# An encoder layer with 32 experts: six of twelve residual tiles stay on chip, and the ring of expert weights has eight places in place of ten

## Chip, cores, metric

The kernel runs on one NeuronCore of a Trainium2 chip. The metric is device time in microseconds (us) of one execution. All matrix work is in float32; where the code says "split", a float32 matrix is taken apart into a rounded part (hi, type fp32r) and the rest (lo), and three products of such parts stand for the one product.

## The reference, cut down

One layer of an encoder is applied to two sequences of 512 and 1024 tokens with 1024 features (1536 tokens, twelve tiles of 128). It is a mixer, a cross-attention to a memory, and a mixture of experts, each added to a residual h:

```python
h = x
h = h + parallel_mixer(rmsnorm(h, g_mix), ...)
h = h + memory_cross_attention(rmsnorm(h, g_xattn), ...)
h = h + hierarchical_moe(rmsnorm(h, g_moe), ...)
return rmsnorm(h, g_final)

def hierarchical_moe(hn, w_rg, w_re, w_gate, w_up, w_down):
    # top-1 of 4 groups, then top-2 of its 8 experts, 32 experts in all
    hg = jnp.einsum('nd,edf->nef', xf, w_gate)     # each expert 1024 x 128
    hu = jnp.einsum('nd,edf->nef', xf, w_up)       # 1024 x 128
    act = jax.nn.silu(hg) * hu * gates[..., None]
    out = jnp.einsum('nef,efd->nd', act, w_down)   # 128 x 1024
```

## The kernel before

All stages up to the experts leave the residual in one SBUF buffer, `H = at(0, NT, D)`: twelve tiles of 4 KB in each partition, at 0 to 48 KB, tile t at 4t KB. After the cross-attention's output is added to tile t, that tile is normalised (`norms` of kind "moe"), stored as rows to DRAM (`xn_moe`), turned and put through the router. When all twelve are through, a table of rows is made, and the experts begin.

**Expert blocks.** Each of the 32 experts first gets one block of up to 128 rows. Rows that did not fit go to overflow blocks afterwards; this input needs seven of them. POOL gathers the rows of block b from `xn_moe` into a ring of `RING = 6` places and scatters the result of block b to `y_tok` in DRAM. In each of the first 32 blocks TensorE runs, in this order, the turning of the next block's rows (L2280), 24 matmuls for gate and up (L571 to L573), `down(b - 1)` (L2314), and the turning of the activation (L2307). ScalarE, in block e - 1, makes the hi part of expert e's gate and up weights (`split_expert`, two instructions of L561), and only behind that comes `silu(e - 1)` (L1323). VectorE makes the lo part of the first half, waits for the silu, multiplies (L1867), and makes the lo part of the second half (L566). `gate_up(e)` on TensorE waits for that last lo part.

**The ring of weights.** Expert e uses place e % `W_RING`. A place holds 12 KB in each partition: gate and up, 8 KB, and down, 4 KB. Three DMAs of 512 KB fill it, all from SyncE's queue (SP), all counted on one semaphore of the place, and `split_expert` waits for all three:

```python
act.wait_ge(w_e_here[e % W_RING], 48 * (e // W_RING + 1))
```

Where the places lie overlaps with other buffers: of the ten, those at 0, 12, 24 and 36 KB lie on H (three tiles each). Experts 0 to 9 are loaded ahead of the expert stage, each as soon as what its place overlaps is done with. From then on the loop in the SP program reloads a place when its reader is done: gate and up when `gate_up` of the place's former expert has ended (`gu_done`), down when its `down` has (`y_done`). SP works strictly in its program's order. Every overflow block loads the weights of its expert again, into the place that `OVER_SLOTS` names, once `down` of the block six before it is done.

**Kept rows.** Since weights overwrite H, SP first copies each tile of H to DRAM (`keep_rows`, L793, `h_kept`), and reads all twelve back after the overflow loads (L850), for the final stage, which adds the experts' rows (`y_tok`, two per token, with their gates) to H and does the last RMSNorm, some tiles on VectorE and some on TensorE.

Of the kernel before, what the change touches and what calls it, by code (L numbers as in the profile page):

```python
# [11 lines left out]
P = 128  # L12
D = 1024
KT = D // P
SEQ_P, SEQ_S = 512, 1024
T = SEQ_P + SEQ_S
NT = T // P
# [28 lines left out]
NBLK = NE + NOVER  # L46
TG = 4
RING = 6
W_RING = 10
OVER_SLOTS = (2, 6, 8, 9, 0, 1)  # L50
AHEAD = 6
EARLY = 4
N_EARLY = 2 * EARLY * P
# [6 lines left out]
def hymba_encoder(nc, a, y_prompt, y_sample):  # L60
    ctx = ExitStack()
    with ctx:
        def sem(name):
            return ctx.enter_context(nc.semaphore(name))
# [6 lines left out]
        def at(kb, *shape, dt=F32):  # L71

            used[0] += 1
            base = nc.sbuf_base + (-nc.sbuf_base) % 32
            return nc.alloc_sbuf_tensor_at(f"at_{kb}_{used[0]}".replace(".", "_"), [P, *shape], dt, offset=base + int(kb * 1024))[:]
# [3 lines left out]
        def dram(name, shape, dt=F32):  # L79
            return nc.dram_tensor(name, shape, dt, kind="Internal").ap()  # L80
# [4 lines left out]
        rpb_pad = dram("rpb_pad", [NH * 15, 96])  # L85
        xn_moe = dram("xn_moe", [T, D])
        y_tok = dram("y_tok", [N_EARLY + 2 * T, D])
        h_kept = dram("h_kept", [T, D])
        xT_hi_all, xT_lo_all = dram("xT_hi_all", [P, KT, T]), dram("xT_lo_all", [P, KT, T])


# [47 lines left out]
        H = at(0, NT, D)  # L139
# [74 lines left out]
        iota_p = at(187, P)  # L214
        iota_blk = at(187.5, NBLK)

        slots_kb = [48, 60, 108, 0, 12, 24, 84, 36, 72, 96]
        w_gu = [at(kb, 2, KT, FE) for kb in slots_kb]
        w_gu_lo = [at(kb, 2, KT, FE, dt=F32R) for kb in slots_kb]
        w_dn = [at(kb + 8, D) for kb in slots_kb]  # L220
# [60 lines left out]
        n_sq, n_eps, n_rs, n_ready, nt_done, nt_evac = (sem(n) for n in ("n_sq", "n_eps", "n_rs", "n_ready", "nt_done", "nt_evac"))  # L281
        xn_stored = [sem(f"xn_stored_{n}") for n in range(4)]
        h_moved = sem("h_moved")
# [8 lines left out]

        w_e_here = [sem(f"w_e_here_{n}") for n in range(W_RING)]
        xg_here = [sem(f"xg_here_{n}") for n in range(RING)]
        xgt_done, xg_hi, xg_lo, gu_done, e_silu, e_act, act_turned, act_evac, y_done, y_evac_s, y_evac_v = (
            sem(n) for n in ("xgt_done", "xg_hi", "xg_lo", "gu_done", "e_silu", "e_act", "act_turned", "act_evac",
                             "y_done", "y_evac_s", "y_evac_v"))
# [30 lines left out]
        TPC = CH // P  # L328
# [103 lines left out]
        for k, st in enumerate(stages):  # L432
            ready = [("pre", n) for n in range(4, len(norms)) if pre_at[n] == k]
            order += [("sq", n) for n in range(4, len(norms)) if sq_at[n] == k]
            if st[0] == "T" and norms[st[1]][0] == "h":
                t = norms[st[1]][1]
# [22 lines left out]
        n_norms = {g: n for n, g in enumerate(norms)}  # L459
# [18 lines left out]
        def overflow_blocks(eng, body):  # L478

            used = eng.value_load(over_n[0:1, 0:1], min_val=0, max_val=NOVER)  # L480
            with eng.Fori(0, NOVER // RING) as i:
                with ExitStack() as nested:
                    for n in range(RING):
                        nested.enter_context(eng.If(used > RING * i + n))
                        body(NE + RING * i + n, n % 2, n, i, NE // 2 + RING // 2 * i + n // 2)

        def over_weights(n, i):

            slot = OVER_SLOTS[n]
            return slot, len(range(slot, NE, W_RING)) + i  # L490

# [115 lines left out]
        def _(sp):  # L607
# [165 lines left out]
            def load_gate_up(e, n):  # L773
                one = slice(e, e + 1) if isinstance(e, int) else bass.ds(e, 1)
                sp.dma_start(w_gu[n][:, 0], a["w_exp_gate"][0, one].rearrange("e (p k) f -> p (e k) f", p=P)).then_inc(w_e_here[n], 16)
                sp.dma_start(w_gu[n][:, 1], a["w_exp_up"][0, one].rearrange("e (p k) f -> p (e k) f", p=P)).then_inc(w_e_here[n], 16)

            def load_down(e, n):
                one = slice(e, e + 1) if isinstance(e, int) else bass.ds(e, 1)
                sp.dma_start(w_dn[n], a["w_exp_down"][0, one].rearrange("e p d -> (e p) d")).then_inc(w_e_here[n], 16)  # L780
# [9 lines left out]

            def keep_rows(t):
                sp.wait_ge(mm_evac, n_groups["xo", t, 1] + 1)
                sp.dma_start(h_kept[t * P:(t + 1) * P], H[:, t]).then_inc(h_moved, 16)  # L793

            def load_expert(e):
                load_gate_up(e, e % W_RING)
                load_down(e, e % W_RING)

# [1 line left out]
                for row in (N_EARLY + k * T, k * EARLY * P):  # L800
                    sp.dma_start(y_tok[row:row + EARLY * P], a["x_prompt"][0][0:EARLY * P]).then_inc(y_filled, 16)

            for t in range(2 * TPC):
                keep_rows(t)
            sp.wait_ge(mm_done, n_groups["o", NCH - 1, XH - 1] + 1)
            for e in range(3):
                load_expert(e)
            sp.wait_ge(h_moved, 16 * 2 * TPC)
            sp.wait_ge(n_ready, n_norms["moe", 2] + 1)
            load_expert(3)  # L810
            sp.wait_ge(n_ready, n_norms["moe", 5] + 1)
            load_expert(4)
            keep_rows(8)
            sp.wait_ge(h_moved, 16 * 9)
            sp.wait_ge(n_ready, n_norms["moe", 8] + 1)
            load_expert(5)
            for t in (9, 10, 11):
                keep_rows(t)
            sp.wait_ge(mm_done, n_groups["xo", NT - 1, 1] + 1)
            load_expert(6)  # L820
            sp.wait_ge(h_moved, 16 * NT)
            sp.wait_ge(n_ready, n_norms["moe", 11] + 1)
            load_expert(7)
            sp.wait_ge(mm_done, len(groups))
            for j in range(4):
                sp.wait_ge(xn_stored[j], 16 * NT // 4)
            load_expert(8)
            load_expert(9)


            for e in range(W_RING, NE):
                sp.wait_ge(gu_done, e - W_RING + 1)
                load_gate_up(e, e % W_RING)
# [11 lines left out]
                load_down(e, slot)  # L845

            overflow_blocks(sp, load_overflow)
            sp.wait_ge(y_done, 28)
            for t in range(NT):
                sp.dma_start(H[:, t], h_kept[t * P:(t + 1) * P]).then_inc(h_moved, 16)  # L850
            sp.dma_start(gf_row, a["g_final"].partition_broadcast(P)).then_inc(consts_here, 16)

            def load_y(t):
# [518 lines left out]
        def _(dve):  # L1372
# [301 lines left out]
            for what, n in order:  # L1674
# [10 lines left out]
                elif what == "pre":  # L1685
                    dve.wait_ge(n_rs, n + 1)
                    kind, t = norms[n]
# [6 lines left out]
                elif what == "T":  # L1694
                    kind, t = norms[n]
# [10 lines left out]
                elif what == "mm":  # L1706
# [3 lines left out]
                    if kind == "xo":  # L1710
                        t, half = which
# [189 lines left out]


            dve.wait_ge(consts_here, 16 * 7)
            dve.wait_ge(h_moved, 16 * 2 * NT)

            def add_experts(t):
                y_landed(dve, t)
# [31 lines left out]
        def _(pe):  # L1939
# [226 lines left out]
            for what, n in stages:  # L2166
# [28 lines left out]
                elif what == "mm":  # L2195
# [31 lines left out]
                    elif kind == "xo":  # L2227
                        t, half = which
# [6 lines left out]
                    else:  # L2235
                        t = which[0]
# [7 lines left out]
                elif what == "S":  # L2244
                    c, t, hp = n // 8, (n % 8) // 2, n % 2
# [89 lines left out]
            pe.wait_ge(table_ready, 4)  # L2335
            overflow_blocks(pe, overflow)

            pe.wait_ge(h_moved, 16 * 2 * NT)
            for m, t in enumerate(BY_PE):
                if m >= 3:  # L2340
                    pe.wait_ge(f_out, with_halves(BY_PE[m - 3]))
# [38 lines left out]
```

## Time and profile before

| what | value |
|---|---|
| median of 3 runs | 1213.64 us (1212.94 to 1214.68) |
| the profiled execution's own time | 1212.87 us |
| its span, first to last instruction | 1211.2 us |
| mean granted TensorE clock | 0.981 of full speed |
| TensorE matmuls busy | 1139.3 us, 94% of the span |
| VectorE, ScalarE, GpSimd busy | 642.2, 470.1, 234.6 us |
| moved by DMA | 226.59 MB |

The span is the profiled execution's instructions from first to last; 1.7 us of its time lie outside. Times of events in the text below are counted from the start of the span. The stretches that matter here are: cross-attention and routing up to about 914, expert blocks 0 to 31 from 915 to 1108, seven overflow blocks to 1159, the final stage to 1211. Busy shares average over stages with different limits; which wait ends last has to be read from each stage.

### The profile page before, as it was taken

The numbers are of one execution on the slowest core, as the hardware profiler recorded it, in microseconds if no ns is written. First come the engines' busy times: TensorE is split into PE (matmuls) and PEld (weight loads), VectorE is DVE, ScalarE is ACT, GpSimd is POOL, SyncE is SP. The second block draws the span as 40 slices with busy tenths as digits, with TensorE's granted clock in tenths as the row PEclk, the third lists the DMA queues.
The fourth block names the chain that finished last, engine by engine and source line by source line (L and its number), as shares of the span: only waits on it lengthen the run. The fifth ranks groups of instructions, "written<-read, shape, count | busy, mean of one in ns | idle before, by whom it ended". The sixth has DMA issues, their size and how long they took to land.

```text
span 1211.2 us, 18987 instructions
## 1 busy us (share of the span) xinstructions
PE 1139.3 (94%) x6854; PEld 912.2 (75%) x6854; DVE 642.2 (53%) x1244; ACT 470.1 (39%) x982; POOL 234.6 (19%) x337
## 2 busy tenths in 40 slices
PE   6999999999998999999999999999986999999956
PEld 5888888878885666888898787778775788887732
DVE  6333333212116896323565663754577998885256
ACT  6233333211015785111332433544224666774223
POOL 3322322200000001000100100100022334454344
PEclk9999999999999999999999999999996999999979
DMA  9573553833158425523222001912796999989967
GB/s 318 133 256 114 145 166 96 296 93 95 46 113 218 110 53 180 174 73 94 62 75 70 1 11 73 317 70 92 307 343 246 373 369 354 357 299 355 406 257 272
DMA packets 108428, 226.59 MB, mean 187 GB/s; under 512 B 28854, under 2 KB 48318, under 8 KB 108222
## 3 DMA queue, kind: packets, MB, share of 16 engines
q1 hardware_dynamic: 83822, 167.86, 40.9%
q0 software_dynamic: 17856, 43.02, 10.8%
q10 hardware_dynamic: 6672, 14.69, 3.8%
q8 instruction: 47, 0.77, 0.3%
q14 instruction: 31, 0.25, 0.1%
HBM read 180.89 MB, written 69.78 MB: 207 GB/s over the span
## 4 chain that ended last, share of the span: by engine, by line
PE 85%; DMA 3%; DVE 3%; ACT 2%; issue 2%; SPq 2%; POOL 1%; DVEq 0%; POOLq 0%; ACTq 0%
PE bank L571 18%; PE bank L573 18%; PE bank L572 18%; PE bank L2314 6%; PE bank L2242 3%; PE bank L2280 3%; PE bank L2111 3%; PE bank L2097 2%; PE bank L2084 2%; PE bank L2300 2%; PE bank L2251 2%; PE bank L2176 1%; DMA at<-v_att 1%; PE bank L1946 1%; PE bank L2022 1%
## 5 line engine op out<-in xcount | busy, mean ns | idle before, releaser
L571 PE MATMUL bank<-at,at 128*128 128x512 f32 (+1 forms) x1192 | 441.1, 370 | 5.3 <-DVE at L566 2.8
L573 PE MATMUL bank<-at,at 128*128 128x512 f32 (+1 forms) x1192 | 431.0, 362 | 0.0
L572 PE MATMUL bank<-at,at 128*128 128x512 f32 (+1 forms) x1192 | 430.5, 361 | 0.0
L571 PEld LDWEIGHTS bank<-at,at 128*128 128x128 f32 x1192 | 225.6, 189 | 40.8 <-DVE at L566 3.6
L573 PEld LDWEIGHTS bank<-at,at 128*128 128x128 f32 x1192 | 225.4, 189 | 34.6
L572 PEld LDWEIGHTS bank<-at,at 128*128 128x128 f32 x1192 | 225.8, 189 | 32.2
L566 DVE TENSOR_TENSOR at<-at,at 128x1024 fp32r<-128x1024 f32 (+2 forms) x162 | 180.7, 1129 | 104.3 <-ACT at L561 101.6
L561 ACT ACTIVATE at<-at 128x1024 fp32r<-128x1024 f32 (+2 forms) x162 | 154.4, 988 | 167.9 <-DVE at L1522 49.0
L894 POOL TENSOR_TENSOR at<-at 128x1 f32<-128x1 f32 x88 | 24.2, 275 | 557.9 <-ACT at L1253 282.3
L2314 PE MATMUL bank<-at,at 128*128 128x512 f32 x156 | 74.2, 597 | 3.3 <-ACT at L1327 3.3
L990 POOL DMA_INDIRECT y_tok<-at,at x39 | 39.5, 1013 | 133.0 <-DVE at L1872 99.0
L983 POOL DMA_INDIRECT at<-xn_moe,at x45 | 59.6, 1324 | 21.5 <-issue 20.8
L1166 ACT ACTIVATE at<-at,at 128x256 f32<-128x256 f32 (+1 forms) x96 | 51.4, 537 | 29.3 <-DVE at L1490 29.1
L896 POOL TENSOR_TENSOR at<-at 128x1 f32<-128x1 f32 x88 | 55.0, 625 | 6.9
L2280 PEld LDWEIGHTS bank<-at,at 128*128 128x128 f32 x320 | 40.5, 193 | 14.0 <-issue 8.0
L1490 DVE CUSTOM_DVE_ANT_0 at<-bank,at 128x256 f32<-128x256 f32 (+1 forms) x96 | 41.1, 466 | 18.0 <-PE bank L2084 17.4
L2280 PE MATMUL bank<-at,at 128*128 128x128 f32 x320 | 44.0, 282 | 7.1 <-DMA at<-xn_moe,at 5.6
L1856 DVE TENSOR_TENSOR at<-bank,at 128x512 fp32r<-128x512 f32 x64 | 41.3, 685 | 12.8 <-ACT at L1314 12.7
L1332 ACT ACTIVATE at<-bank 128x512 f32<-128x512 f32 x39 | 23.3, 598 | 62.9 <-PE bank L2314 56.0
L2097 PEld LDWEIGHTS bank<-at,at 128*128 128x128 f32 x224 | 24.0, 142 | 28.0 <-ACT at L1166 25.1
L2314 PEld LDWEIGHTS bank<-at,at 128*128 128x128 f32 x156 | 26.7, 190 | 24.0 <-issue 18.8
L2242 PE MATMUL bank<-at,at 128*128 128x36 f32 (+1 forms) x240 | 43.8, 339 | 0.0
(215 smaller groups left out, 1316.2 us busy)
## 6 DMA issues: line engine op xcount, KB each, us to landing
at<-in_w_exp_gate SPq DMA_DIRECT2D x39, 512.0 KB, 7.3
at<-in_w_exp_up SPq DMA_DIRECT2D x39, 512.0 KB, 10.3
at<-in_w_exp_down SPq DMA_DIRECT2D x39, 512.0 KB, 12.7
at<-y_tok SPq DMA_DIRECT2D x24, 512.0 KB, 10.4
at<-in_w_in SPq DMA_DIRECT2D x6, 1024.0 KB, 11.5
xT_hi_all<-at POOLq DMA_DIRECT2D x12, 512.0 KB, 3.9
xT_lo_all<-at POOLq DMA_DIRECT2D x12, 512.0 KB, 5.7
at<-xT_hi_all SPq DMA_DIRECT2D x3, 2048.0 KB, 10.1
```

The lines of the kernel that those rows point to most:

```text
L561: nc.scalar.activation(hi, x, ACT.Copy).then_inc(hi_made, 1)
L566: nc.vector.tensor_tensor(lo, x, hi.bitcast(F32), ALU.subtract).then_inc(lo_made, 1)
L571: nc.tensor.matmul(out, w_hi, x_hi, start=(k == 0), stop=False)
L572: nc.tensor.matmul(out, w_lo, x_hi, start=False, stop=False)
L573: last = nc.tensor.matmul(out, w_hi, x_lo, start=False, stop=(k == len(terms) - 1))
L896: pool.tensor_tensor(rs[:, col:col + 1], ms_eps[:, col:col + 1], neg_half, ALU.pow).then_inc(out_sem, 1)
L983: pool.indirect_dma_start(out=x_g[b % RING], out_offset=None, in_=xn_moe, in_offset=bass.IndirectOffsetOnAxis(ap=slot_src[:, b:b + 1], axi ...
L1166: nc.scalar.activation(p, p, ACT.Exp, bias=na_st[:, 2 * (s % 2) + n:2 * (s % 2) + n + 1], scale=-1.0, accum_out=na_st[:, 4 + 2 * (s % 2) + ...
L2097: last = nc.tensor.transpose(bank[4 + n][:, k * P:(k + 1) * P], na_p[s % 2][:, n, k * P:(k + 1) * P], ident)
L2242: mm = nc.tensor.matmul(b if kind == "route" else b[:], w, x, start=(k == 0), stop=(k == len(steps) - 1))
L2280: mm = nc.tensor.transpose(bank[k // 4][:, (k % 4) * P:(k % 4 + 1) * P], x_g[n].rearrange("p (q k) -> p k q", k=KT)[:, k], ident)
L2314: mm = nc.tensor.matmul(bank[5 + k][:], act_T[j], w_dn[slot][:, k * HALF:(k + 1) * HALF], start=True, stop=True)
```

## The change

H stays where it is. Its tiles 0 to 5 (0 to 24 KB) are no longer overlapped by weights: the places at 0 and 12 KB are gone, and eight are left. The copies of tiles 0 to 5 to DRAM and back go with them. Ahead of the expert stage eight experts are loaded instead of ten. The copy of tile 8, of which SP waited behind five loads, now stands behind three.

```diff
-W_RING = 10
-OVER_SLOTS = (2, 6, 8, 9, 0, 1)
+W_RING = 8
+OVER_SLOTS = (0, 1, 2, 4, 6, 7)
+KEPT = 6
...
-        h_kept = dram("h_kept", [T, D])
+        h_kept = dram("h_kept", [T - KEPT * P, D])
...
-        slots_kb = [48, 60, 108, 0, 12, 24, 84, 36, 72, 96]
+        slots_kb = [48, 60, 108, 24, 84, 36, 72, 96]
...
-            for t in range(2 * TPC):
+            for t in range(KEPT, 2 * TPC):
                 keep_rows(t)
             sp.wait_ge(mm_done, n_groups["o", NCH - 1, XH - 1] + 1)
             for e in range(3):
                 load_expert(e)
-            sp.wait_ge(h_moved, 16 * 2 * TPC)
-            sp.wait_ge(n_ready, n_norms["moe", 2] + 1)
+            keep_rows(8)
+            sp.wait_ge(h_moved, 16 * (9 - KEPT))
+            sp.wait_ge(n_ready, n_norms["moe", 8] + 1)
             load_expert(3)
-            sp.wait_ge(n_ready, n_norms["moe", 5] + 1)
-            load_expert(4)
-            keep_rows(8)
-            sp.wait_ge(h_moved, 16 * 9)
-            sp.wait_ge(n_ready, n_norms["moe", 8] + 1)
-            load_expert(5)
             for t in (9, 10, 11):
                 keep_rows(t)
             sp.wait_ge(mm_done, n_groups["xo", NT - 1, 1] + 1)
-            load_expert(6)
-            sp.wait_ge(h_moved, 16 * NT)
+            load_expert(4)
+            sp.wait_ge(h_moved, 16 * (NT - KEPT))
             sp.wait_ge(n_ready, n_norms["moe", 11] + 1)
-            load_expert(7)
+            load_expert(5)
             sp.wait_ge(mm_done, len(groups))
             for j in range(4):
                 sp.wait_ge(xn_stored[j], 16 * NT // 4)
-            load_expert(8)
-            load_expert(9)
+            load_expert(6)
+            load_expert(7)
...
-            sp.wait_ge(y_done, 28)
-            for t in range(NT):
-                sp.dma_start(H[:, t], h_kept[t * P:(t + 1) * P]).then_inc(h_moved, 16)
+            sp.wait_ge(y_done, 30)
+            for t in range(KEPT, NT):
+                sp.dma_start(H[:, t], h_kept[(t - KEPT) * P:(t - KEPT + 1) * P]).then_inc(h_moved, 16)
...
-            dve.wait_ge(h_moved, 16 * 2 * NT)
+            dve.wait_ge(h_moved, 16 * 2 * (NT - KEPT))
...
-            pe.wait_ge(h_moved, 16 * 2 * NT)
+            pe.wait_ge(h_moved, 16 * 2 * (NT - KEPT))
```

## Rows read from the trace of the kernel before

**Rows 1.** The page: each engine's busy us, its share of the span, instructions.
```profile
PE 1139.3 (94%) x6854; PEld 912.2 (75%) x6854; DVE 642.2 (53%) x1244; ACT 470.1 (39%) x982; POOL 234.6 (19%) x337
```

**Rows 2.** Windows: engines' busy us, then granted clock, DMA share, GB/s.
```profile
855.00:884.00 29.00, 27.06 (x169) 23.93 (x170) 17.95 (x53) 6.68 (x13) 1.49 (x4) 1.00 0.93 362
...
930.00:960.00 30.00, 29.24 (x189) 23.10 (x188) 27.99 (x46) 19.76 (x36) 7.74 (x8) 1.00 0.81 300
960.00:990.00 30.00, 30.00 (x204) 25.00 (x204) 28.09 (x48) 20.59 (x37) 10.70 (x11) 1.00 1.02 387
...
1020.00:1050.00 30.00, 30.00 (x205) 24.94 (x203) 25.63 (x37) 21.62 (x38) 15.38 (x12) 1.00 0.95 365
...
1066.00:1080.00 14.00, 14.00 (x89) 10.97 (x88) 11.78 (x15) 9.07 (x17) 7.83 (x6) 1.00 0.84 316
1080.00:1090.00 10.00, 10.00 (x73) 8.72 (x72) 8.06 (x12) 7.83 (x14) 5.44 (x4) 1.00 0.68 247
1090.00:1106.00 16.00, 16.00 (x110) 13.24 (x109) 11.88 (x16) 9.08 (x17) 8.18 (x7) 1.00 0.98 348
```

**Rows 3.** Timeline of SP's queue: start us, us of issuing, line, transfer.
```profile
930.15 0.33 SPq L775 DMA_DIRECT2D at<-in_w_exp_gate  x1
...
1035.39 4.81 SPq L780 DMA_DIRECT2D at<-in_w_exp_down  x1
...
1058.79 2.10 SPq L780 DMA_DIRECT2D at<-in_w_exp_down  x1
1060.93 2.30 SPq L775 DMA_DIRECT2D at<-in_w_exp_gate  x1
...
1065.45 1.21 SPq L780 DMA_DIRECT2D at<-in_w_exp_down  x1
1085.81 0.35 SPq L775 DMA_DIRECT2D at<-in_w_exp_gate  x1
```

**Rows 4.** DMA issues, landing us last: down 1035.39; down 1058.79 and 1065.45; gate 1060.93.
```profile
at<-in_w_exp_down SPq DMA_DIRECT2D x1, 512.0 KB, 26.9
...
at<-in_w_exp_down SPq DMA_DIRECT2D x1, 512.0 KB, 24.5
...
at<-in_w_exp_gate SPq DMA_DIRECT2D x1, 512.0 KB, 9.4
```

**Rows 5.** Timeline of ACT, DVE and PE around the weights of experts 24 and 31.
```profile
1059.35 2.03 ACT L561 ACTIVATE at<-at 128x1024 fp32r<-128x1024 f32 x2
...
1098.46 2.03 ACT L561 ACTIVATE at<-at 128x1024 fp32r<-128x1024 f32 x2
1100.72 0.28 ACT L1323 ACTIVATE at<-bank 128x128 f32<-128x128 f32 x1 [0.23 <-PE bank L573]
...
1101.23 1.22 DVE L566 TENSOR_TENSOR at<-at,at 128x1024 fp32r<-128x1024 f32 x1
...
1103.16 0.36 PE L571 MATMUL bank<-at,at 128*128 128x256 f32 x1
```

**Rows 6.** SP around the copy of tile 8: its timeline row, and SP's waits.
```profile
863.56 1.77 SPq L793 DMA_DIRECT2D h_kept<-at  x1
...
SPq L775 <- DMA h_kept<-at: 18.4, 2, 16.9
```

**Rows 7.** Overflow: down loads issued about 1086.73 and 1103.48, landing; chain's first overflow matmuls.
```profile
at<-in_w_exp_down SPq DMA_DIRECT2D x1, 512.0 KB, 10.0
...
at<-in_w_exp_down SPq DMA_DIRECT2D x1, 512.0 KB, 12.7
...
1110.83 3.45 PE bank L2300 x16
...
1117.81 3.45 PE bank L2300 x16
```

**Rows 8.** Reading H back: timeline of SP's queue, and the window of 1150 to 1155.
```profile
1120.79 11.84 SPq L850 DMA_DIRECT2D at<-h_kept  x12
...
1150.00:1155.00 5.00, 5.00 (x19) 3.66 (x20) 0.91 (x2) 0.60 (x1) 1.18 (x2) 1.00 0.62 237
```

More of the change, by code:

```diff
@@ L792, in keep_rows @@
                 sp.wait_ge(mm_evac, n_groups["xo", t, 1] + 1)
-                sp.dma_start(h_kept[t * P:(t + 1) * P], H[:, t]).then_inc(h_moved, 16)
+                sp.dma_start(h_kept[(t - KEPT) * P:(t - KEPT + 1) * P], H[:, t]).then_inc(h_moved, 16)
             def load_expert(e):
```

## The prediction

> **What bounds the kernel now.** I read the page first: TensorE is busy for 94% of the span [rows 1]. Then the windows. From 960 to 1106 TensorE has no idle time at all, so an expert block costs what its matmuls cost: the weights of experts 24 and 31 are split at 1059.35 and 1098.46, seven blocks apart, 5.59 us each [rows 5]. The same windows show the second thing to see: DMA is at a share of 0.95 to 1.02 and 365 to 387 GB/s for most of that time [rows 2]. So the expert stage is bound by TensorE with DMA just below it, and what keeps DMA hidden is the lead of the weight loads. I looked at that lead in the timeline of SP's queue and in the landing times [rows 3, 4].
>
> Expert 27's down load is issued at 1035.39 and lands 26.9 us later, at 1062.3. Those of 30 and 31 are issued at 1058.79 and 1065.45 and land 24.5 us later, at 1083.3 and 1090.0. That is (1090.0 - 1062.3) / 4 = 6.9 us for an expert's weights, and 6.7 for the last one, against 5.59 us for a block of TensorE. The stream of weights is slower than its reader, and the kernel lives on the lead that ten places give.
>
> The deadline of the last expert is worked out backwards from the timeline [rows 5]. `gate_up(31)` starts at 1103.16. VectorE's last lo part for it ends at 1101.23 + 1.22 = 1102.45, 0.7 us sooner. ScalarE's split of expert 31 starts at 1098.46 and ends at 1100.49, and the silu behind it starts 0.23 us later only because TensorE is not done. So the weights may land 0.7 + 0.2 = 0.9 us after 1098.46, at 1099.4, before anything moves. They land at 1090.0: the lead is 9.4 us, less than two blocks. Experts 28, 29, 30 have deadlines 5.59 us apart: 1082.6, 1088.2, 1093.8.
>
> **The change part by part.**
>
> *Six writes and six reads of H go.* Each is 0.524 MB, 3.15 MB each way. The writes were issued during cross-attention, where nothing of TensorE's chain waits for them. The twelve reads are issued from 1120.79 on, under overflow blocks that TensorE fills, and DMA already falls to a share of 0.62 at 1150 to 1155, before the final stage [rows 8]. What is taken away was hidden at both ends: 0 us. If that cover were gone, 3.15 MB at 365 GB/s would be 8.6 us each way.
>
> *Two loads fewer ahead of the experts.* The old loads of experts 3 and 4 vanish from the stretch of 855 to 884 [rows 2]. The copy of tile 8 was issued at 863.56, and SP waited up to 16.9 us for it [rows 6]. It is now behind three loads instead of five, and lands up to 3.15 MB / 362 GB/s = 8.7 us sooner. Behind that wait stand the load of expert 3 and the copies of tiles 9 to 11. They may start sooner, but expert 3 isn't split until four blocks in, so the gain is nothing. All that follows (experts 4 to 7 in place of 6 to 9) keeps the same waits on TensorE and VectorE, so the first gather meets the same queue: 0 us.
>
> *The moved stream.* In the loop the load of e waits for expert e - 8 instead of e - 10. The first is issued by the same event as before, the end of `gate_up(0)` at 930.15 [rows 3]; it was expert 10 and is now expert 8. From there on the SP program issues the same bytes on the same events, with the numbers moved by two, and gathers and scatters beside them are unchanged. So I take the landing times of before and give them to experts two lower: 28 lands when 30 did, 29 when 31 did. The last two, 30 and 31, have no forerunner. They follow without a pause, since DMA was left idle only after this point (share 0.84 and then 0.68 [rows 2], with SP issuing nothing from 1065.45 to 1085.81 [rows 3]). At 6.7 us each they land at 1096.7 and 1103.4, at 6.9 at 1096.9 and 1103.8.
>
> Against the deadlines: expert 28 at 1083.3 - 1082.6 = 0.7 us late, 29 at 1090.0 - 1088.2 = 1.8, 30 at 2.9 to 3.1, 31 at 4.0 to 4.4. Lateness does not add up, since one late block moves all later deadlines; the last one is the stall, 4.2 us in all, in four pieces of about 1 us. When TensorE waits, its gathers and scatters wait too. They are what is left of the 365 GB/s after 1.57 MB in 6.9 us, 228 GB/s: 137 GB/s, or 0.4 us of DMA given back for each us of stall. With about 2 us stalled ahead of the last landing that is 0.7 us. Sum: 4.2 - 0.7 = +3.5 us. Bounds: below, 0, if the last two loads fit wholly in the idle share; above, 4.4 without relief and up to about 6 if the pace is 7.6 us for the last two.
>
> At the same load, gate lands 9.4 us after its issue and down 24.5 [rows 4], although gate of expert 31 is issued after down of expert 30: landing is not in order of issue. The Trainium skill ("DMA: Bandwidth & Descriptors", "Why a DMA increments its semaphore by 16 and not by 1") says that a DMA runs on up to 16 engines that finish independently, and that only the full count means all has landed. By the 9.4 us, expert 31 would be there long before 1099.4 and the sum would be 0; by the last of the three, which is what `split_expert` waits for, it is +3.5. The rows of the down loads decide, and I take the second.
>
> *Overflow.* `OVER_SLOTS` names other places, but each load waits for the same `y_done` as before. The first overflow load, at 1085.81, landed by about 1096.7, and its matmuls started at 1110.83 [rows 3, 7]. Now it queues behind expert 31: 1103.5 + 6.7 = 1110.2, against 1110.8 + 3.5 = 1114.3. The margin shrinks from 14 us to 4 us, but TensorE takes 7.0 us for such a block (1110.83 to 1117.81 [rows 7]), as long as a load needs, so it isn't used up. 0 us. The wait `y_done` 30 in place of 28 stands behind the last overflow load, which needed 33 already.
>
> *Final stage.* Its bytes before the end: two experts (3.15 MB) later, six reads (3.15 MB) fewer. Even: 0 us.
>
> The profiled execution would go from 1212.87 to 1216.4. The median lies 0.8 us above it, so 1213.64 + 3.5 = 1217.1 us.
>
> **The rivals.** What measurement can tell from no change is 0.2%, 2.4 us.
>
> *The two loads fit in the gap: no change.* From 1066 to 1090 DMA has idle share of 0.16 x 14 + 0.32 x 10 = 5.4 us [rows 2], and by bytes at the 387 GB/s of 960 to 990 two experts need 8.1 us: 1090.0 + 8.1 = 1098.1, in time for 1099.4. With up to 1 us of stall at 28 and 29 it stays at 1213.6 to 1215. Against it: the pace of 6.7 to 6.9 us at full share is that of the same bytes with gathers beside them. The Trainium skill (same page, "Bandwidth") measured 425 GB/s for a core that streams alone; by it two experts would take 7.4 us and be in time too. No window of the expert loop shows it; the most there is 387.
>
> *More than the last four: the overflow loads come late as well.* Their margin is 4 us. If landings spread by 2 us more for each of the last two experts, both the stall and the overflow blocks take it: 3.5 + 4 = about 1221. For it: landing grew from 10.0 to 12.7 us even behind an idle queue [rows 7]. Against it: gathers end as overflow begins.
>
> *Faster.* Ahead of the experts DMA runs at 0.93 from 855 to 884 [rows 2], with stores of `xn_moe` in the same engines, and TensorE is idle for 1.9 us there. If those idle times hang on late stores and loads, taking 3.15 MB out gives up to 1.9 us: 1211.7. It decides only if the last experts land in time too. Nothing in that stretch is shown waiting for DMA except SP itself.
>
> **How the numbers follow.** Forecast 0.61, at 1217.1, own range 1215.2 to 1219. No change 0.24. Overflow late too 0.09. Faster 0.06. The forecast's lower edge falls within 0.2% about one time in twenty. So slower 0.67, same 0.26, faster 0.07. The range of 8 in 10 reaches down into "no change" and up towards the third case: 1213.3 to 1220.3.
>
> **What would show it.** In the changed kernel: DMA share near 1 from 1066 to 1090; ScalarE's L561 waiting for `at<-in_w_exp_down` in the blocks of experts 28 to 31, PE idle for 3 to 4 us in about 1080 to 1110, none before; the loads of 30 and 31 landing near 1097 and 1103; the first overflow matmul near 1114; the stretch before 930 unchanged. Wrong would be: no idle PE in the loop; idle PE in earlier blocks, which would mean that the stream isn't the old one moved by two; or a changed stretch before 930.

## The result and the profile after

| what | before | changed |
|---|---|---|
| median of 22 runs each | 1213.62 us (1211.96 to 1217.95) | 1216.17 us (1212.41 to 1220.13) |
| ratio of the two | | 1.002, interval 1.0012 to 1.0027 |
| the profiled execution | 1212.87 us, span 1211.2 | 1215.17 us, span 1213.3 |
| moved by DMA | 226.59 MB | 220.30 MB |

The changed kernel is slower by 2.5 us, 0.2%, where the prediction had 3.5 us; its median lies in the forecast's own range (1215.2 to 1219). It moves 6.29 MB less and is still slower. The page of the changed kernel, its span, busy times and bytes, against [rows 1]:

```profile
span 1213.3 us, 18973 instructions
...
PE 1140.6 (94%) x6854; PEld 913.1 (75%) x6854; DVE 643.9 (53%) x1244; ACT 470.5 (39%) x982; POOL 228.1 (19%) x337
...
DMA packets 106701, 220.30 MB, mean 182 GB/s; under 512 B 28663, under 2 KB 48127, under 8 KB 106495
```

TensorE does the same work in a span that is 2.1 us longer. The windows say where DMA is used otherwise, with the columns of [rows 2]:

```profile
855.00:884.00 29.00, 26.85 (x168) 23.76 (x169) 17.93 (x53) 6.87 (x13) 1.48 (x4) 1.00 0.88 326
930.00:960.00 30.00, 29.24 (x189) 23.03 (x187) 27.86 (x46) 19.70 (x37) 7.59 (x8) 1.00 0.84 301
...
1066.00:1080.00 14.00, 14.00 (x89) 11.01 (x89) 11.68 (x16) 9.21 (x17) 7.96 (x6) 1.00 1.00 361
1080.00:1090.00 10.00, 10.00 (x73) 8.71 (x72) 6.82 (x10) 6.67 (x12) 4.05 (x4) 1.00 0.92 354
1090.00:1106.00 16.00, 15.34 (x97) 11.76 (x96) 12.46 (x17) 10.78 (x20) 4.05 (x4) 1.00 0.95 335
```

From 1066 to 1090, DMA's share was 0.84 and 0.68; it is 1.00 and 0.92. The idle room is filled, and TensorE has idle time behind it, 16 - 15.34 = 0.66 us from 1090 to 1106. Since the ends of matmuls are modelled, short idle times can be missing there; ScalarE's timeline shows the stall more sharply. These are the splits of experts 28 to 31, one row each:

```profile
1082.11 2.01 ACT L562 ACTIVATE at<-at 128x1024 fp32r<-128x1024 f32 x2
...
1089.10 2.00 ACT L562 ACTIVATE at<-at 128x1024 fp32r<-128x1024 f32 x2 [1.52 <-DMA at<-in_w_exp_down]
...
1095.46 2.00 ACT L562 ACTIVATE at<-at 128x1024 fp32r<-128x1024 f32 x2 [1.89 <-DMA at<-in_w_exp_down]
...
1101.12 2.01 ACT L562 ACTIVATE at<-at 128x1024 fp32r<-128x1024 f32 x2 [1.18 <-DMA at<-in_w_exp_down]
```

Undisturbed they would stand 5.59 us apart, at 1087.4, 1093.0 and 1098.6 for the last three. The waits of 925 to 1115 that end on a weight load or on the split behind it (us in total, number, longest):

```profile
DVE at L567 <- ACT at L562: 5.7, 5, 2.0
ACT at L562 <- DMA at<-in_w_exp_down: 4.6, 3, 1.9
```

The kernel before has no wait of ScalarE for `in_w_exp_down` there. A word on that name: the three loads of a place count on one semaphore, 16 counts each, and the profile gives the first 16 counts to gate, the next to up and the last to down, in the order of issue. So the landing that it prints for a down load is the moment of the 48th count, when all three are there, and that is what the split waits for. The landing printed for gate is only the 16th of the 48 counts, whichever loads they came from.

SP's queue shows the loads moved (against [rows 3]), and the landings behind three of its rows are 27.1 us for the down load of expert 29, 24.4 for expert 30 and 23.9 for expert 31:

```profile
930.29 0.33 SPq L776 DMA_DIRECT2D at<-in_w_exp_gate  x1
...
1061.94 4.73 SPq L781 DMA_DIRECT2D at<-in_w_exp_down  x1
...
1071.08 1.84 SPq L781 DMA_DIRECT2D at<-in_w_exp_down  x1
...
1077.17 1.87 SPq L781 DMA_DIRECT2D at<-in_w_exp_down  x1
1085.95 0.35 SPq L776 DMA_DIRECT2D at<-in_w_exp_gate  x1
```

So 29 lands at 1061.94 + 27.1 = 1089.0, 30 at 1095.5, 31 at 1101.1, each at the start of its split. Last, the chain: the first overflow matmuls and the last ones of the final stage, against [rows 7]:

```profile
1112.51 3.45 PE bank L2296 x16
...
1199.11 3.45 PE bank L2348 x8
```

The first was at 1110.83: +1.68. The last was at 1196.89: +2.2 (2.1 in the span). These 2.2 us are: 0.15 us that the expert stage begins later, 1.5 us of stall at experts 29 to 31, 0.1 in the overflow blocks, 0.45 in the final stage.

**How profiles are compared below.** The stretch ahead of the experts varies from one execution to the next: the loop's first load is issued between 929.2 and 932.1 in the twelve profiles, against 930.15 in that of the kernel before. So each profile is given its shift: the start of the split of expert 12 (990.97 in the kernel before, 991.12 in the changed one, shift +0.15). The stall in the loop is the first overflow matmul minus 1110.83 minus the shift. The ratios take in all runs of both kernels and are not the quotient of the two medians.

### The profile page after: what moved, and what is told of

Same layout as the page of the kernel before. It is cut to its first block, busy times and chain, and to the rows that moved or that the text cites. A ratio compares the mean times of both kernels' runs of the same rounds, so it can differ in the third digit from the quotient of the medians.

```text
span 1213.3 us, 18973 instructions
## 1 busy us (share of the span) xinstructions
PE 1140.6 (94%) x6854; PEld 913.1 (75%) x6854; DVE 643.9 (53%) x1244; ACT 470.5 (39%) x982; POOL 228.1 (19%) x337
## 2 busy tenths in 40 slices
DMA packets 106701, 220.30 MB, mean 182 GB/s; under 512 B 28663, under 2 KB 48127, under 8 KB 106495
## 4 chain that ended last, share of the span: by engine, by line
PE 84%; DMA 4%; issue 3%; ACT 2%; DVE 2%; SPq 2%; POOL 1%; DVEq 0%; POOLq 0%; ACTq 0%
PE bank L572 18%; PE bank L574 17%; PE bank L573 17%; PE bank L2310 5%; PE bank L2238 3%; PE bank L2107 3%; PE bank L2276 2%; PE bank L2093 2%; PE bank L2080 2%; DMA at<-in_w_exp_down 2%; PE bank L2296 2%; PE bank L2247 2%; PE bank L2348 2%; PE bank L2172 2%; DMA at<-y_mix 1%
## 5 line engine op out<-in xcount | busy, mean ns | idle before, releaser
L979 POOL DMA_INDIRECT at<-xn_moe,at x45 | 55.6, 1236 | 21.5 <-issue 21.2
```

Of the source, the lines that this page charges most:

```text
L979: pool.indirect_dma_start(out=x_g[b % RING], out_offset=None, in_=xn_moe, in_offset=bass.IndirectOffsetOnAxis(ap=slot_src[:, b:b + 1], axi ...
```

## The experiments

The theory (A, where the expectations use letters): the lead of the weight loads is what eight places take away. The stall comes where the last landing of an expert's three loads passes the deadline of its split. The copies of H are worth nothing to either end. Against it stand: the copies count (ahead of the experts or in the final stage), or it is not the lead but the load of DMA in the loop.

**The number of places.** Nine places, three tiles kept (the loads ahead of the experts follow suit):

```diff
-W_RING = 8
-OVER_SLOTS = (0, 1, 2, 4, 6, 7)
-KEPT = 6
+W_RING = 9
+OVER_SLOTS = (5, 7, 8, 0, 1, 2)
+KEPT = 3
...
-        slots_kb = [48, 60, 108, 24, 84, 36, 72, 96]
+        slots_kb = [48, 60, 108, 12, 24, 84, 36, 72, 96]
```

> Nine places for expert weights, tiles 0 to 2 stay in SBUF, tiles 3 to 11 are copied out and read back. Theory A (the cost is the lead of the weight stream): the last expert lands one item of the stream later than with ten places, near 1095.5 in place of 1090.0, and the deadline of its split is 1099.4. So there is no stall: no idle TensorE in blocks 25 to 31, the first overflow matmul at 1111, and a time within 0.5 us of the kernel before. Theory B (the cost comes with the number of places or copies changed, by other placement or other traffic): half the change gives half the cost, +1.3 us.

Measured: 1213.24 us against 1212.77 of the kernel before on the same chip, ratio 1.0006 (0.9996 to 1.0015). ScalarE does not wait for weights, and the first overflow matmul is at 1110.36 with shift -0.47: stall 0. One place fewer is covered by the lead.

Seven places, with only tiles 6 to 8 copied:

```diff
-W_RING = 8
-OVER_SLOTS = (0, 1, 2, 4, 6, 7)
+W_RING = 7
+OVER_SLOTS = (4, 5, 6, 0, 1, 2)
...
-        slots_kb = [48, 60, 108, 24, 84, 36, 72, 96]
+        slots_kb = [48, 60, 108, 24, 84, 72, 96]
...
-            for t in range(KEPT, NT):
+            for t in range(KEPT, KEPT + 3):
```

> Seven places, tiles 0 to 5 and 9 to 11 stay in SBUF, only 6 to 8 are copied out and read back. Theory A: the stream goes on for one more item of about 5.6 to 6.4 us behind the landing at 1101.1, so expert 31 lands near 1107, and TensorE stalls about 5 us more than with eight places, in the blocks from about expert 27 on, less the relief from gathers and scatters that wait too: +6 to +8 us against the kernel before. Theory B, in proportion to the places: 3/2 of 2.5 us, +3.8 us; if fewer copies gave something back, less.

Measured: 1218.61 us, ratio 1.0044 (1.0028 to 1.0059). Its wait for weights in the same stretch, and three of the rows of ScalarE's timeline:

```profile
ACT at L562 <- DMA at<-in_w_exp_down: 10.3, 6, 3.0
```

```profile
1064.28 2.00 ACT L562 ACTIVATE at<-at 128x1024 fp32r<-128x1024 f32 x2 [2.87 <-DMA at<-in_w_exp_down]
...
1089.63 2.00 ACT L562 ACTIVATE at<-at 128x1024 fp32r<-128x1024 f32 x2 [3.02 <-DMA at<-in_w_exp_down]
...
1105.68 2.01 ACT L562 ACTIVATE at<-at 128x1024 fp32r<-128x1024 f32 x2
```

The stall begins at expert 23 (its split at 1056.93) instead of 29, and the last two splits are in time again. First overflow matmul at 1117.83, shift +1.8: 5.2 us in the loop. From ten to seven places the medians are 0, +0.5 (not told from nothing), +2.5 and +5.8 us. That the cost starts only at the eighth is what a lead with a threshold gives, and not what a cost per byte gives.

**Is it the wait for the down load?** Eight places, but down is counted on semaphores of its own, `split_expert` waits for gate and up alone, and `down` waits for its own load:

```diff
...
-                act.wait_ge(w_e_here[e % W_RING], 48 * (e // W_RING + 1))
+                act.wait_ge(w_e_here[e % W_RING], 32 * (e // W_RING + 1))
...
-            def down(b, j, slot):
+            def down(b, j, slot, n_loads):
+                pe.wait_ge(w_d_here[slot], w_d_base[slot] + 16 * (n_loads + 1))
```

> Eight places as in the changed kernel, but the down weights are counted on semaphores of their own, and the split of gate and up waits for those two alone; the matmul for down waits for its own. Theory A: gate and up of expert 31 are issued some 2 to 5 us ahead of down and land 2 to 4 us ahead of it, so the splits of experts 29 to 31 start on time; down itself is needed 8 us later than the split. ScalarE no longer waits for a weight load, TensorE is idle 0 to 0.5 us in the loop, and the time is that of the kernel before, within 0.8 us. Theory B (traffic or placement): no difference from the changed kernel, +2.5 us. If the landing is spread so much between DMA engines that gate and up come as late as down, A gives +2 us as well, and the profile shows ScalarE still waiting.

Measured: 1214.19 us, ratio 1.0015 (1.0003 to 1.0028), where the changed kernel stands at 1.002 (1.0012 to 1.0027). The intervals overlap, so the times alone do not tell the two kernels apart; the profile does. It has the span (1211.2) and the first overflow matmul (1110.83) of the kernel before, shift 0: no stall. What is left of the wait:

```profile
ACT at L564 <- DMA at<-in_w_exp_up: 0.9, 2, 0.6
```

Gate and up still keep the splits of experts 29 and 30 waiting, 0.2 and 0.6 us, which the 0.9 us of slack take up. The split of expert 31 begins at 1099.23 instead of 1098.46, after a wait that the profile gives to no load: 0.1 us more would have been a stall. Gate and up of expert 30 are there at 1093.61, where all three loads were at 1095.46 in the changed kernel. What was gained by not waiting for down is 1.3 and 1.7 us at experts 29 and 30, less the shifts, just enough here.

The same with SP's order by need, gate and up of e + 1 ahead of down of e:

```diff
...
-            for e in range(W_RING, NE):
-                sp.wait_ge(gu_done, e - W_RING + 1)
-                load_gate_up(e, e % W_RING)
-                sp.wait_ge(y_done, e - W_RING + 1)
-                load_down(e, e % W_RING)
+            for e in range(W_RING, NE + 1):
+                if e < NE:
+                    sp.wait_ge(gu_done, e - W_RING + 1)
+                    load_gate_up(e, e % W_RING)
+                if e > W_RING:
+                    sp.wait_ge(y_done, e - W_RING)
+                    load_down(e - 1, (e - 1) % W_RING)
```

> Eight places, down counted apart, and SyncE issues gate and up of expert e + 1 ahead of down of expert e, so that gate and up stand 0.5 MB further ahead in the stream, 2 us at its pace. Theory A (the cost is the lead of what the split waits for): ScalarE waits 0 to 0.3 us for weights, the first overflow matmul at 1110.8, and the median within 0.8 us of the kernel before, at or below the one with down merely apart, whose ScalarE still waited 0.9 us for up and whose median was 1.4 us above before. Down of expert 31 now lands last, near 1101, and is needed near 1106, so it adds nothing. Theory B, that what remained in that run was something else than waits for weights: again +1.4 us.

Measured: 1213.65 us against 1213.10, ratio 0.9999 (0.999 to 1.0008). No wait of ScalarE for weights at all; first overflow matmul at 1109.88, shift -0.97: stall 0. With the same eight places and the same bytes, the cost is gone. So the cause is the lead, the time between the landing that the split waits for and the split's deadline, and not the number of places in itself. How much of it is the count and how much the order is not shown: the new order also lets SP finish issuing sooner, its last load of the loop at 1071.68 instead of 1080.08 with down merely apart, and the order alone was not tried.

**The changed kernel once more**, beside the last one on the same chip:

> The changed kernel itself once more, on the same chip as the next three, so that small differences to them are not differences of chips. Both theories: +2 to +3 us against the kernel before; in the profile ScalarE waits for at<-in_w_exp_down at the splits of experts 29 to 31, 4 to 5 us in all, and the first overflow matmul starts 1.5 to 2 us later than at 1110.8.

Measured: 1215.54 us, ratio 1.0017 (1.0008 to 1.0025). Its final stage is as long as that of the kernel before. Its stall is smaller, 1112.62 - 1110.83 - 0.97 = 0.8 us, and so are its waits:

```profile
ACT at L562 <- DMA at<-in_w_exp_down: 3.5, 3, 1.6
```

**The copies.** Eight places with all twelve tiles copied and read back (`KEPT = 0`, nothing else differs from the changed kernel):

> Eight places as in the changed kernel, but all twelve tiles are copied out and read back as before. Theory A (copies hidden at both ends): the same as the changed kernel, +2.5 us. In the changed kernel the overflow weights land up to 8 us later than before (1139 in place of 1131), so the six more reads, 3.15 MB or 8 us, may reach into the start of the final stage: then up to +5 us. Theory B in the form that the copies of tiles 0 to 5 cost time in the kernel before, hidden in the balance: clearly over +2.5 us, with the loss in the stretch before 930.

Measured: 1219.23 us, ratio 1.0058 (1.0044 to 1.0072), +6.5 us where the changed kernel had +2.5. The loop is that of the changed kernel (first overflow matmul 1112.40, shift -0.36: stall 1.9 us). What differs is the end. SP's queue, VectorE's first row of the final stage, and windows of 1150 to 1160:

```profile
1124.67 14.54 SPq L846 DMA_DIRECT2D at<-h_kept  x12
...
1140.41 11.27 SPq L854 DMA_DIRECT2D at<-y_tok  x8
```

```profile
1167.55 0.87 DVE L1825 TENSOR_SCALAR at<-at,at 128x128 f32<-128x128 f32 x4 [6.23 <-DMA y_tok<-at,at]
```

```profile
1150.00:1155.00 5.00, 4.63 (x22) 3.31 (x21) 1.67 (x3) 1.68 (x4) 0.69 (x1) 1.00 1.01 390
1155.00:1160.00 5.00, 4.63 (x23) 3.22 (x21) 0.98 (x2) 1.15 (x3) 2.03 (x2) 1.00 0.49 189
```

The same rows of the changed kernel:

```profile
1125.71 7.03 SPq L846 DMA_DIRECT2D at<-h_kept  x6
...
1133.96 11.41 SPq L854 DMA_DIRECT2D at<-y_tok  x8
```

```profile
1165.16 0.87 DVE L1825 TENSOR_SCALAR at<-at,at 128x128 f32<-128x128 f32 x4 [3.73 <-DMA y_tok<-at,at]
```

```profile
1150.00:1155.00 5.00, 4.63 (x23) 3.27 (x22) 1.67 (x3) 1.68 (x4) 0.80 (x1) 1.00 0.33 123
1155.00:1160.00 5.00, 4.63 (x23) 3.33 (x21) 0.98 (x2) 1.15 (x3) 2.02 (x2) 1.00 0.12 40
```

And that of the kernel before:

```profile
1163.39 0.87 DVE L1829 TENSOR_SCALAR at<-at,at 128x128 f32<-128x128 f32 x4 [3.63 <-DMA y_tok<-at,at]
```

In the kernel with all copies and the changed one, the last scatter is issued at nearly the same time (1162.17 and 1162.29). With twelve reads the `y_tok` loads start 6.45 us later and DMA is still full at 1155; VectorE starts the final stage 2.4 us later after a wait that is 2.5 us longer, and the last matmuls are at 1202.20 instead of 1199.11: 3.1 us. So with eight places, in which the overflow weights land late, the six reads are worth about 3 us.

Is that so without the stall too? The ordered kernel with `KEPT = 0`:

> Eight places with down apart and the order changed (no stall in the loop), but all twelve tiles copied out and read back. It separates the two costs of the run with eight places and all copies, +6.5 us. If the six more reads push the final stage, as its profile suggests (VectorE's first instruction of that stage 2.4 us later, and 0.7 us more up to the end), this run has no stall in the loop and +2.5 to +4 us in all. If that run's extra cost hung on the stall, this one gives the time of the kernel before.

Measured: 1215.88 us against 1212.52, ratio 1.0025 (1.0016 to 1.0034), against 0.9999 with six reads. No wait of ScalarE for weights; first overflow matmul at 1112.37, shift +1.53: stall 0. The final stage begins late again:

```profile
1166.79 0.87 DVE L1829 TENSOR_SCALAR at<-at,at 128x128 f32<-128x128 f32 x4 [5.38 <-DMA y_tok<-at,at]
```

Less the shift that is 1165.26, 1.9 us later than in the kernel before, and the last matmuls, at 1201.14, are 2.7 us later less the shift. The price of the reads needs no stall, only the stream moved by two.

Now the writes alone. Ten places; the copies of tiles 0 to 5 aren't written, and the rows of tiles 6 to 11 are read back in their place, so the residual of six tiles is left out of the result. SP's waits on `h_moved` follow suit:

```diff
...
-            for t in range(2 * TPC):
+            for t in range(6, 2 * TPC):
                 keep_rows(t)
...
-                sp.dma_start(H[:, t], h_kept[t * P:(t + 1) * P]).then_inc(h_moved, 16)
+                sp.dma_start(H[:, t], h_kept[(t % 6 + 6) * P:(t % 6 + 7) * P]).then_inc(h_moved, 16)
```

> The kernel before without the copies of tiles 0 to 5 to DRAM; all twelve are still read back, for tiles 0 to 5 the rows of tiles 6 to 11 are read, so the residual of tiles 0 to 5 is wrong in the result. It shows what six writes cost ahead of the experts. My theory: nothing, 0.0 us, within what can be told (0.2%), since no wait of TensorE's chain ends with them. The other: up to 1.9 us faster, the idle time of TensorE from 855 to 884, if late stores cause it.

Measured: 1213.45 us against 1213.10, ratio 1.0001 (0.9991 to 1.0011). The writes cost nothing ahead of the experts, to within 1.3 us. With that falls the rival that taking them out makes the kernel faster.

**Ten places and more bytes.** If all that counts is when weights land, ten places must stall too, once the stream is late by as much. Six DMAs of 512 KB, from one place in DRAM to another, behind the down loads of experts 25 to 30:

```diff
...
+                if 25 <= e < 31:
+                    n = e - 25
+                    sp.dma_start(spare[n * P:(n + 1) * P], a["x_sample"][0][n * P:(n + 1) * P]).then_inc(y_filled, 16)
```

> The kernel before, with ten places and all its copies, and six more transfers of 512 KB (DRAM to DRAM, a part of x to a spare tensor) from SyncE's queue, one behind each down load of experts 25 to 30: the 3.15 MB that the change moves into the loop, without the shorter lead. Expert 31 then lands near 1098 in place of 1090, against a deadline of 1099.4. Theory A: in the loop 0 to 0.5 us. The same bytes also push the overflow weights and the reading back of H later, as in the run with all copies, so the final stage may start 0 to 3 us late: +0 to +3 us in all, with none of it before 1110. Theory C (bytes in the loop cost by themselves, whatever the lead): a stall in the loop of 1.5 us or more before the first overflow matmul, as in the changed kernel. A copy within DRAM may hold the DMA engines longer than a load; then the last weights come after 1099.4 and some stall shows for A too.

Measured: 1219.56 us against 1213.10, ratio 1.0037 (1.0022 to 1.0051); four of its six runs are near 1219.6 and two near 1216, so its median says little. It stalled more than was meant, for expert 31 landed 6 us later than the 1098 that was expected:

```profile
1095.64 2.00 ACT L562 ACTIVATE at<-at 128x1024 fp32r<-128x1024 f32 x2 [0.85 <-DMA at<-in_w_exp_down]
...
1104.22 2.00 ACT L562 ACTIVATE at<-at 128x1024 fp32r<-128x1024 f32 x2 [3.42 <-DMA at<-in_w_exp_down]
```

Expert 31 landed at 1104.2 instead of 1090.0, 12.5 us later less the shift of +1.7, for 3.15 MB. The deadline, with the shift, was 1101.1; it was 3.1 us late, and the first overflow matmul, at 1117.12, is 4.6 us late less the shift. A landing past its deadline stalls a kernel of ten places as well. But since the landing did pass its deadline, both theories give a stall, and this run doesn't set them apart; so half of it was tried, behind experts 27 to 29 (`27 <= e < 30`):

> As the run with ten places and six more transfers, with three of them, behind the down loads of experts 27 to 29. Six delayed expert 31 by 14 us, so three should delay it by about 7: it lands near 1097, 2 us ahead of its deadline of 1099.4. Theory A (a stall only where the landing passes the deadline): ScalarE does not wait for weights, the first overflow matmul starts as in the kernel before, +0 to +1.5 us in all from a later final stage. Theory C (bytes in the loop cost in proportion): half of what the six cost, a stall of about 2 us in the loop and +3 us in all.

Measured: 1214.92 us against 1212.52, ratio 1.0015 (1.0005 to 1.0025). The splits of experts 30 and 31 are in time, at 1094.81 and 1100.40 with shift +1.94, and the stall in the loop is 0. DMA's added load alone does nothing there. What the three copies cost shows in the final stage:

```profile
1167.32 0.87 DVE L1834 TENSOR_SCALAR at<-at,at 128x128 f32<-128x128 f32 x4 [5.64 <-DMA y_tok<-at,at]
```

That is 2.0 us late less the shift, with the same wait for the last scatter that six more reads gave. Three more copies in the loop and six more reads behind it, two different ways to make DMA's work end later, show in the same row.

The kernels side by side. The two columns on the right come from one profile each, in us:

| kernel | places | median, before's beside it | ratio (interval) | loop stall | final stage starts late by, less the shift |
|---|---|---|---|---|---|
| changed | 8 | 1216.17, 1213.62 | 1.0020 (1.0012 to 1.0027) | 1.5 | 1.6 |
| changed again | 8 | 1215.54, 1213.10 | 1.0017 (1.0008 to 1.0025) | 0.8 | 1.0 |
| nine places | 9 | 1213.24, 1212.77 | 1.0006 (0.9996 to 1.0015) | 0.0 | 0.0 |
| seven places | 7 | 1218.61, 1212.77 | 1.0044 (1.0028 to 1.0059) | 5.2 | 5.2 |
| down apart | 8 | 1214.19, 1212.77 | 1.0015 (1.0003 to 1.0028) | 0.0 | 0.1 |
| down apart, ordered | 8 | 1213.65, 1213.10 | 0.9999 (0.9990 to 1.0008) | 0.0 | 0.1 |
| all copies | 8 | 1219.23, 1212.77 | 1.0058 (1.0044 to 1.0072) | 1.9 | 4.5 |
| ordered, all copies | 8 | 1215.88, 1212.52 | 1.0025 (1.0016 to 1.0034) | 0.0 | 1.9 |
| six writes less | 10 | 1213.45, 1213.10 | 1.0001 (0.9991 to 1.0011) | 0.0 | 0.2 |
| six copies in the loop | 10 | 1219.56, 1213.10 | 1.0037 (1.0022 to 1.0051) | 4.6 | 4.9 |
| three copies in the loop | 10 | 1214.92, 1212.52 | 1.0015 (1.0005 to 1.0025) | 0.0 | 2.0 |

No version beats the kernel before. The best of eight places, down apart and ordered, equals it.

## Why the prediction was right in its kind and too large in its size

**Bound and deadlines: right.** The deadline of a split was worked out as 0.9 us after its undisturbed start. In the changed kernel expert 31 landed at 1101.1, against 1099.4 + 0.15: 1.55 us late, and the stall is 1.5. Expert 30 landed 1.5 us late and 29 0.7, and both are pieces of the same 1.5, since, as predicted, only the last lateness counts. The seven-place kernel follows the same rule: its last late landing is that of expert 29 at 1095.26, 5.3 us past the deadline with the shift, and its stall is 5.2. The kernel with six copies follows it less exactly (3.1 us late, 4.6 us of stall; it also has six waits of ScalarE for scatters, 9.7 us in all, where the changed kernel has two, 5.3 us).

**The stream moved by two: right as a mechanism, and the term that was mis-sized.** The step that failed in size is "at 6.7 us each they land at 1096.7 and 1103.4". They landed at 1095.5 and 1101.1. Two parts make up the 2.3 us. The whole stream came about 1 us ahead of its map: expert 28 at 1082.1, not 1083.3, and 29 at 1089.0, not 1090.0; and so 28 was just in time where 0.7 us late was predicted. And the last two followed 6.4 and 5.6 us apart instead of 6.7. The stall was to be 4.2 us with 0.7 given back; it was 1.5 us in this profile and 0.8 and 1.9 us in the two others of the same loop.

The prediction took 6.7 us from expert 31 in the kernel before and called it the pace at full share. But that load landed while DMA's share was 0.68 [rows 2], and SP had issued nothing behind it until 1085.81 [rows 3]. So 6.7 us was not the pace of a full DMA, nor that of a load with more behind it. What did change is what ran beside the loads. The queue of gathers and scatters moved 1.74 MB from 1077 to 1089 in the changed kernel and 0.85 MB from 1089 to 1101, while the last two experts landed. It moved as little there in the kernel before, 0.97 MB, without any stall: from block 26 on, POOL gathers for the overflow blocks. The prediction had the gathers and scatters at 137 GB/s throughout, and its 0.7 us of relief depended on the stall. That the lighter traffic is why the last two came faster fits these numbers; no run tested it. Why the whole stream came 1 us ahead isn't known either. From 1025 to 1079 SP issues without a gap of more than 0.4 us, so the loads of that stretch no longer hang on the events that the prediction moved them by.

**The idle share of 1066 to 1090 as room: partly the rival "no change".** DMA did use it, at a share of 1.00 and 0.92. The rival expected 1098.1 for the last landing, the forecast 1103.4, and 1101.1 lies between them. Neither price was right; the deadline at 1099.4 decides, and on it the forecast's side was right. The idle share was also not all room: expert 31's loads needed until 1090.0 in the kernel before although DMA stood at 0.68 from 1080 to 1090 [rows 2]. A landing waits for the last of its counts, and the share is a mean over 16 engines. The windows from 1066 to 1106 moved 335 to 361 GB/s, gathers and scatters with the weights. By the 425 GB/s that the Trainium skill gives for a core that streams alone ("DMA: Bandwidth & Descriptors", "Bandwidth") expert 31 would, by estimate, have been in time; no window of a profile here shows such a rate in the loop.

**The last of three landings: right, but the 9.4 us of gate were misread.** The split started with the last of the three landings, and with down out of the wait the profile shows no stall. The rule of the Trainium skill that only the full count means that all has landed ("DMA: Bandwidth & Descriptors", "Why a DMA increments its semaphore by 16 and not by 1") agrees with these rows. But the 9.4 us after gate's issue are the 16th of 48 counts, and not the landing of gate. The counts of expert 31 in the kernel before run from 1066.2 to 1090.0, with the 16th at 1070.3. In the run with down apart, where down has a count of its own, gate and up of experts 29 and 30 were complete only 1.3 and 1.7 us ahead of all three in the changed kernel, less the shifts. So the prediction's alternative, in which gate and up of expert 31 are there long before 1099.4 and the sum is 0, had no ground in that row.

**Copies, writes: right.** Nothing ahead of the experts changed but the loads' own times, and ten places without six of the writes run as fast as before, to within 1.3 us.

**Copies, reads: "hidden at both ends: 0" holds only for the old stream; "even" in the final stage was right.** The prediction priced the reads at 0 in one step and used them as a credit against two later experts in another. The second is what the runs show: six reads more cost 2.7 to 3.1 us in the final stage once the stream is two experts late, with a stall and without one. Without that credit the change would have cost 6.5 us (1219.23 against 1212.77). Of the 0.45 us that the changed kernel lost in the final stage, the repeat shows nothing, so it isn't put to the change.

**Overflow: right.** First load landed at 1107.0, with its matmuls at 1112.51; the margin was to shrink from 14 to 4 us and was 5.5. Overflow blocks keep their 7.0 us, except that the whole ran 0.1 us longer.

**What is left open.** The medians differ by 2.5 us, twice; the two profiles account for 2.0 and 0.9 us less their shifts. The stall varies between executions, and two or three profiles don't give its mean. The kernel with down apart has no stall in its profile and yet a ratio of 1.0015 with the lower end at 1.0003. In that profile expert 31 came within 0.1 us of a stall, so other executions may well stall; whether they do, or something else is in it, isn't known. Nor is it known what makes the stretch ahead of the experts differ by up to 2.9 us from run to run.

## What to carry to other kernels

Before a prefetch ring is made smaller, work out its lead at the last use: the deadline of the wait that guards it, less the landing of the last transfer that the wait counts. It was 9.4 us here for a block of 5.6 and an expert's three loads of 6.7; nine places cost nothing that could be told, eight cost 2.5 us and seven 5.8 us by the medians. If the lead is too short, look at what the wait counts and at the order of the queue: to wait for the two loads that are needed instead of three, and to issue them in the order of need, gave back together all that the two places had cost. And when loads share a semaphore, the profile can't tell their landings apart: only the last of them is sure. Last, a transfer that is hidden is hidden by a margin that other parts of the change may spend, so its price is to be taken again in the new schedule.

## What the runs showed of the hardware that was not expected

The 16 counts of one load do not come together. In the run with down apart, the recorded counts of expert 30's down load of 512 KB run from 1078.3 to 1095.6, 17 us, after its issue at 1071.97. A consumer waits for the last. So loads can be late while DMA's mean share is far below 1, as in the kernel before from 1080 to 1090 (0.68). How long that takes depends on what is still under way: the last count of an expert came 24.5 us after the issue of its down load in the full stream [rows 4], and 10.0 us after it when SP had issued nothing for 19 us before [rows 7].

A copy of 512 KB from DRAM to DRAM held up the stream only a little more than a load into SBUF. Six of them made expert 31 12.5 us late, 2.1 us each. The six loads that two places fewer put ahead of it made it 11.0 us late in the changed kernel (1101.1 less the shift, against 1090.0), 1.8 us each.

The time in which SP issues one load of 512 KB is not constant: in the changed kernel it took 4.73 us for a down load at 1061.94, and 0.47 at 1086.88, after 6.9 us in which SP had issued nothing. That the full queue holds SP fits the rows of 1025 to 1079, which follow one another with gaps of at most 0.4 us, but no run tested it.
